# Seven-product units of a squared-ReLU MLP: where relu, squares and low halves stand in the order of two engines

## What is computed

```python
def sq_relu_mlp(h, w_up, w_down):
    return jnp.square(jax.nn.relu(h @ w_up)) @ w_down
...
        x = x + g1 * y_x
        h2 = modulate(rmsnorm(x, norm2_g[l]), sh2, sc2)
        x = x + g2 * sq_relu_mlp(h2, w_up[l], w_down[l])
```

## Time and profile before

| what | value |
|---|---|
| median of 3 runs | 1730.41 us |
| the three runs | 1732.12, 1727.40, 1730.41 us |
| the profiled execution's own time | 1729.16 us |
| its span, first to last instruction | 1727.4 us |
| mean granted TensorE clock | 0.970 |
| busy: TensorE (PE) | 1631.7 us, 94% |
| busy: VectorE (DVE) | 1273.7 us, 74% |
| busy: ScalarE (ACT) | 919.3 us, 53% |
| busy: GpSimd (POOL) | 255.6 us, 15% |
| DMA | 322.89 MB, mean 187 GB/s |

### The profile page before, as it was taken

How to read it: one execution, slowest core, us unless ns; L and a number is a source line. 1 busy time by engine, 2 the same in 40 slices (tenths; PEclk the granted TensorE clock), 3 DMA queues, 4 the chain that set the end, 5 groups by cost and what they waited for, 6 DMA issues and landing times.

```text
span 1727.4 us, 20083 instructions
## 1 busy us (share of the span) xinstructions
PE 1631.7 (94%) x8178; PEld 1321.9 (77%) x8178; DVE 1273.7 (74%) x1457; ACT 919.3 (53%) x1070; POOL 255.6 (15%) x176
## 2 busy tenths in 40 slices
PE   5999998999999898989999999889999999999994
PEld 2768876657988788887988687778888888888883
DVE  7544875877667646474699975479999898999984
ACT  6423235443443524253633234477878888888884
POOL 0000030000037131320000100021221212122110
PEclk9999998999999999999999998999999999999997
DMA  9106721003131223223122110289999999999993
GB/s 383 66 4 245 292 79 74 0 0 144 52 122 67 105 74 104 92 77 118 50 98 74 50 50 30 98 330 411 378 370 375 372 370 370 357 374 360 381 365 116
DMA packets 54482, 322.89 MB, mean 187 GB/s; under 512 B 12529, under 2 KB 13041, under 8 KB 17778
## 3 DMA queue, kind: packets, MB, share of 16 engines
q1 hardware_dynamic: 42192, 304.76, 46.2%
q0 software_dynamic: 9216, 8.43, 2.2%
q10 hardware_dynamic: 2978, 8.37, 1.2%
HBM read 323.60 MB, written 23.07 MB: 201 GB/s over the span
## 4 chain that ended last, share of the span: by engine, by line
PE 79%; DVE 10%; ACT 5%; DMA 3%; issue 2%; SPq 0%; POOL 0%; ACTq 0%; POOLq 0%; DVEq 0%
PE ps L584 25%; PE ps L1437 19%; PE ps L1464 10%; PE ps L763 4%; DVE blo L2274 2%; PE ps L739 2%; PE ps L1326 2%; PE ps L1002 2%; DVE scr L2475 2%; PE ps L796 1%; PE ps L1423 1%; DVE wlo L2165 1%; ACT whi L1515 1%; DMA xT<-in_x 1%; DVE scr L2274 1%
## 5 line engine op out<-in xcount | busy, mean ns | idle before, releaser
L2165 DVE TENSOR_TENSOR wlo<-raw,whi 128x2048 fp32r<-128x2048 f32 x256 | 585.3, 2307 | 146.4 <-ACT whi L1515 146.2
L1515 ACT ACTIVATE whi<-raw 128x2048 fp32r<-128x2048 f32 x256 | 485.2, 1910 | 142.6 <-PE ps L584 41.6
L1437 PE MATMUL ps<-whi,xH 128*128 128x512 f32 x512 | 205.2, 401 | 2.0 <-DVE xL L2274 2.0
L1437 PE MATMUL ps<-whi,xL 128*128 128x512 f32 x512 | 201.3, 393 | 0.0
L1437 PE MATMUL ps<-wlo,xH 128*128 128x512 f32 x512 | 199.9, 390 | 0.0
L584 PE MATMUL ps<-hH,whi 128*128 128x512 f32 x352 | 140.7, 400 | 0.3 <-ACT dmax L1980 0.3
L584 PE MATMUL ps<-hL,whi 128*128 128x512 f32 x352 | 139.2, 395 | 0.0
L584 PE MATMUL ps<-hH,wlo 128*128 128x512 f32 x352 | 139.1, 395 | 0.0
L3210 POOL DMA_INDIRECT sum_scratch<-yb,idt x32 | 51.1, 1595 | 454.6 <-ACT yb L2105 449.3
L1437 PEld LDWEIGHTS ps<-whi,xL 128*128 128x128 f32 x512 | 96.4, 188 | 22.5
L1437 PEld LDWEIGHTS ps<-whi,xH 128*128 128x128 f32 x512 | 96.7, 189 | 21.3 <-DVE xL L2274 2.3
(11 more groups left out here) (514 smaller groups left out, 3533.2 us busy)
## 6 DMA issues: line engine op xcount, KB each, us to landing
raw<-in_experts SPq DMA_DIRECT2D x192, 1024.0 KB, 7.7
raw<-in_streamed SPq DMA_DIRECT2D x92, 1024.0 KB, 4.8
xT<-in_x SPq DMA_DIRECT2D x1, 2048.0 KB, 17.2
h_scratch<-hN ACTq DMA_DIRECT2D x4, 512.0 KB, 2.6
sum_scratch<-xN ACTq DMA_DIRECT2D x1, 2048.0 KB, 13.8
out<-Y SPq DMA_DIRECT2D x4, 512.0 KB, 2.7
ctxT<-in_ctx SPq DMA_DIRECT2D x1, 1024.0 KB, 18.7
Y<-sum_scratch SPq DMA_DIRECT2D x2, 512.0 KB, 5.6
```

Source lines behind the costliest of these rows:

```text
L1437: ins = e.matmul(b.t[:, :], l, w, start=(kk == 0 and i == 0), stop=(kk == 7 and i == 2))
L1515: e.activation(u.hi, u.raw, ACT.Copy).then_inc(*p.inc("hi", n, on="hi"))
L2165: e.tensor_tensor(u.lo, u.raw, u.hi.bitcast(F32), ALU.subtract).then_inc(*p.inc("lo", n, on="lo"))
```

## The change

On ScalarE, relu and squares of unit c move into unit c+1: relu behind high half g+11 of the later unit, the squares behind its `p1s`. The high halves up to g+12 now stand ahead of `p1s`, and those up to g+17 behind the squares. In the fourth unit its own relu and squares follow at the end. On VectorE the low halves go up to g+10 ahead of the unit's first wait, to g+12 behind `u2s` and to g+14 ahead of `c1221`, in place of up to g+17 by the end. TensorE, GpSimd and SyncE are not changed, and no instruction or DMA is added or taken away.

```diff
@@ act_program, mlp
+        def positive(ch, c):
+            p.wait_ge(*done("dve", "c1221", ch, c))
+            e.activation(quad, quad, ACT.Relu).then_inc(*p.inc("r", ch, c))
+
+        def squared(ch, c):
+            p.wait_ge(*done("act", "r", ch, c))
+            p.wait_ge(*done("pe", "chunk", ch - 1))
+            e.activation(UH[:, 2 * c:2 * c + 2, :], scr[:, :, :], ACT.Square).then_inc(*p.inc("uh2", ch, c))
+            e.activation(quad, quad, ACT.Square).then_inc(*p.inc("us", ch, c))
+
         def seven(ch, c, n):
             g = STEP_AT[n]
+            ready(g + 11)
+            if c:
+                positive(ch, c - 1)
+            ready(g + 12)
             p.wait_ge(*done("pe", "block", n, 1))
             if n != U_UP[1][0]:
                 p.wait_ge(*done("dve", "c11", *((ch, c - 1) if c else (ch - 1, 3))))
             copy(p1s, ps["a", ch, c].t[:, 0:256], p.inc("p1s", ch, c))
-            for j in range(6):
-                ready(g + j + 11)
-            p.wait_ge(*done("dve", "c1221", ch, c))
-            e.activation(quad, quad, ACT.Relu).then_inc(*p.inc("r", ch, c))
-            p.wait_ge(*done("act", "r", ch, c))
-            p.wait_ge(*done("pe", "chunk", ch - 1))
-            e.activation(UH[:, 2 * c:2 * c + 2, :], scr[:, :, :], ACT.Square).then_inc(*p.inc("uh2", ch, c))
-            e.activation(quad, quad, ACT.Square).then_inc(*p.inc("us", ch, c))
+            if c:
+                squared(ch, c - 1)
             ready(g + 17)
+            if c == 3:
+                positive(ch, c)
+                squared(ch, c)
@@ dve_program, mlp
         def seven(ch, c, n):
             g = STEP_AT[n]
             a, b, d, f = (ps[x, ch, c].t for x in "abdf")
-            ready(g + 11)
+            ready(g + 10)
             p.wait_ge(*done("pe", "block", n, 1))
             p.wait_ge(*done("act", "p1s", ch, c))
             TT(u2s, a[:, 256:512], p1s, ALU.add, "u2s", ch, c)
@@
                             ALU.add).then_inc(*p.inc("w34", ch, c))
-            ready(g + 13)
             p.wait_ge(*done("dve", "w34", ch, c))
             TT(quad[:, 768:1024], b[:, 0:256], w34[:, 1, :], ALU.add, "c22", ch, c)
-            ready(g + 14)
             p.wait_ge(*done("pe", "block", n, 4))
             TT(quad[:, 0:256], d[:, 0:256], p1s, ALU.add, "c11", ch, c)
-            ready(g + 15)
-            ready(g + 16)
+            ready(g + 14)
             p.wait_ge(*done("pe", "block", n, 6))
             TT(quad[:, 256:768], f[:, :], sqs[:, :], ALU.add, "c1221", ch, c)
-            ready(g + 17)
             if c == 3:
                 lower_pair(ch, c)
```

## The result

The changed kernel takes 1704.82 us (median of 4 runs, 1701.89 to 1705.23), the kernel before 1730.81 beside it: ratio 0.9849, 95% interval 0.9831 to 0.9867. The forecast was 1704.2. Measured again later, it took 1703.87 us beside 1730.67, ratio 0.9842 (0.9828 to 0.9856); one of its six runs, which took 2341.01 us at a granted clock of 0.647, is left out of both.

What follows compares the result with a forecast made beforehand. TensorE carries 79% of the chain; it loses 8.54 + 8.67 + 8.97 = 26.2 us at three up-to-down switches. 1729.16 - 26.2 = 1703.0, and 1704.2 for the median, which lay 1.25 higher; range 1699.5 to 1716.

Steps and rivals of the forecast that it cites:

- The loss of 26.2 us at three switches: Where each chunk's up half ends and down half begins, TensorE idles, then runs slowly: 8.54, 8.67 and 8.97 us.
- the term for the slow matmuls: First 48 down matmuls of each chunk, partly at 1.2 GHz: 2.20, 2.30 and 2.63 us lost.
- 26.2 out, 0 in.: Whole kernel: the loss at the three switches goes, 26.2 us, and the moved work adds nothing.
- the rest moves forward as a block: Behind the sevens stage the chain stays on TensorE, so everything there was to come earlier unchanged.
- T6: Theory of a follow-up, not the prediction: VectorE's shorter reach costs a little, ScalarE's order alone 1 us or more faster.
- The tracing: Hand-traced VectorE times, chunk 1: first down low half at 583.0, wanted 586.35; last UL at 593.9, wanted 594.5.
- GpSimd's fourth sum: In units with sums, VectorE and GpSimd take turns, each turn costing VectorE one GpSimd sum, 1.3 us.
- Margins: Chunk 1: first down low half ready at 583.0 for 586.35; last UL just fits with 0.6 us to spare.
- ScalarE's waits: Sign in the changed profile: ScalarE's relu, which waited 6.64 us for VectorE's additions, waits under 3 us.
- Rival B (half comes): Last low half or first down half late in some chunk, TensorE waits: 1705 to 1718 us, middle 1708; chance 0.19.
- Rival C (VectorE sets the pace): Port shared with GpSimd slows VectorE to 12.8 us a unit against TensorE's 9.86: slower, 1737 us; chance 0.05.

Runs made afterwards that it cites:

- ul_x2: The changed kernel with each UL of the seven-product units made twice, one behind the other: 1706.21 us, ratio 0.986.
- high17: The kernel before with one edit on ScalarE, high half g+17 moved ahead of relu from behind the squares: 1713.95 us, ratio 0.9903.
- dve_only: The kernel before with only VectorE's part of the change, ScalarE keeping its old order: 1715.49 us, ratio 0.991.
- ul_x3: The changed kernel with each UL of the seven-product units made three times: 1730.57 us, ratio 0.9998.
- act_only: The kernel before with only ScalarE's part of the change, VectorE keeping its old order: 1703.73 us, ratio 0.9847; again later 1703.22 us.

## Why the prediction was right, point by point

- **The loss of 26.2 us at three switches.** The idle time and the slow matmuls are gone entirely, at all three. Two switches gave 8.45 each where I had 8.54 and 8.67. From the plain matmuls ahead of the sevens to those behind them (chain pieces at 514.45 and 788.99 before, 514.86 and 763.74 after) 274.5 us have become 248.9, so all three gave 25.7. What was mis-sized is the term for the slow matmuls. I set 13.08 us, which run from the first matmul's start to the end of the last one's record (0.39), against 48 pitches of 0.2267: the 0.16 by which a record is longer than its pitch was counted as loss, 0.5 us for three chunks.
- **"26.2 out, 0 in."** Between the two profiled executions the span fell by 24.2, from 1727.4 to 1703.2, and the medians by 26.0. That the forecast of 1704.2 lies within 0.6 of the measured 1704.82 is in part luck: the interval of the ratio is 3 us wide to each side, and two small errors lie inside it. One is the 0.5 us above. The other is my sentence that the rest moves forward as a block, which was not quite true. Behind the sevens stands a norm with a pause of TensorE, and there the clock was low for longer than before. Stretches before, then after, columns as in the earlier trace rows:

```profile
821.60:824.40 2.80, 2.80 (x14) 2.80 (x14) 0.59 (x2) 0.26 (x1) 0.00 (x0) 0.50 0.02 6
824.40:828.00 3.60, 3.60 (x29) 3.47 (x28) 2.60 (x6) 1.65 (x4) 0.00 (x0) 0.94 0.00 0
```

```profile
796.20:799.00 2.80, 2.80 (x14) 2.80 (x15) 0.59 (x2) 0.26 (x1) 0.00 (x0) 0.50 0.03 6
799.00:802.50 3.50, 3.50 (x20) 3.32 (x20) 2.01 (x5) 1.23 (x3) 0.00 (x0) 0.63 0.00 0
```

  Behind the same first stretch, 29 matmuls pass in 3.6 us before and 20 in 3.5 us after: about 1 us lost in this execution. From the first L692 piece of this norm to the first of L739 the chain takes 7.4 us before and in both profiled executions of ScalarE's order alone, and 8.7 in both of the changed kernel. That is the size of the difference which T6 went after; whether it is more than chance two executions of each do not show.
- **The tracing.** Chunk 1: low half of the first down unit: 583.0 forecast, 580.07 measured. Last UL: 593.9 against 592.06. VectorE's lateness in the second unit: 6.6 us forecast, 3.0 measured (`c1221` ends at 570.10, the next unit's first matmul starts at 567.09). The term that was mis-sized is GpSimd's fourth sum. I let it go ahead of low half g+14 in each unit. In the trace VectorE's next low half, standing ready, went first and took 0.69 us, and the sum took 1.69 where 1.3 is its shortest. So in each of the two units VectorE did not lose a turn of about 1.2 us that I had charged. The price of a turn was right: a UL beside a sum, which the trace of before did not show, took 2.34 us where I had 1.23 to 2.52. In chunk 2, counted from its first product at 630.30, the low half was ready at 32.7 and the last UL at 44.7, forecast 32.5 and 44.3.
- **Margins.** Forecast 3.3 and 0.6 us in chunk 1, measured 6.7 and 2.9. I had the fourth unit's last addition end 3.2 us behind its product; it was 0.9, with VectorE waiting for the product. That the last UL is the narrower one was right, and ul_x2 and high17 show TensorE stopping at exactly that place, k=6.
- **ScalarE's waits.** I said that the relu waits would be under 3 us; the one of the fourth unit is 3.70 in each chunk, because it waits for TensorE's own last product.
- **Rival B (half comes)** did not happen and is what dve_only and high17 do: 15.4 and 16.9 us faster than the 1730.84 beside them.
- **Rival C (VectorE sets the pace)** is real at a distance. It takes 2.5 us more on VectorE per unit, and then the kernel is back at 1730.57. I had its place right, UL at k=6, but looked only at the units with sums. By my own sum VectorE's work in a unit with nothing in its way is 7.6 us; with 2.5 more it is above TensorE's 9.86, so lateness is not made up where GpSimd is idle. In chunk 1 of ul_x3 the last additions end 5.6 us behind their product in the second unit, 5.9 in the third and 7.3 in the fourth; in the changed kernel it is 3.0, 0.9 and 0.9. The Trainium skill (SBUF — State Buffer, "Who interferes with whom") has the pair locked for a whole instruction by the first comer; the rows agree (a UL of one shape takes 1.23 us alone and 2.21 to 2.34 beside a sum).
- **What the prediction did not separate** is the two halves. ScalarE's alone gives the whole gain, VectorE's alone 15.4 us of it, and VectorE's on top of ScalarE's nothing in time.

## What to carry to other kernels

When two engines each show long idle times that end on the other, look at what stands in front of the awaited instruction in its queue: here a 0.6 us conversion stood behind 3 us of work that itself waited. Let work that waits for another engine's result lag by one unit, and put independent work ahead of it. Then measure the room with a repeated instruction: a schedule that gains 26 us and one that gains none lay 2.5 us of VectorE work per unit apart. And look at what a margin hangs on: the rooms of 6.7 and 2.9 us here stayed the same when VectorE had less to do, because each begins with something that VectorE and ScalarE wait for TensorE to finish.

## What was not expected of the hardware

A wait of TensorE of about 2 us brings the clock down in one chunk and not in the next, in one execution. In dve_only it waits the same 1.85 to 1.86 us ahead of each down half. The stretches behind these waits:

```profile
590.00:591.00 1.00, 1.00 (x4) 0.71 (x4) 1.00 (x2) 0.00 (x0) 0.00 (x0) 0.50 0.68 123
...
676.00:680.00 4.00, 3.96 (x17) 3.30 (x18) 3.97 (x6) 0.00 (x0) 0.00 (x0) 1.00 0.70 250
...
684.00:686.00 2.00, 0.50 (x3) 0.07 (x1) 1.19 (x1) 2.00 (x2) 0.14 (x1) 1.00 0.61 254
...
763.00:768.00 5.00, 4.97 (x15) 3.92 (x16) 4.96 (x7) 0.00 (x0) 0.00 (x0) 0.66 0.57 210
```

The granted clock is 0.50 (1.2 GHz) in chunk 1 and 0.66 on the mean in chunk 3, and full in chunk 2; high17's waits of 2.2 us at k=6 were followed by the full clock in all three. In dve_only the low clock cost nothing on balance. At full clock, in chunk 2, TensorE comes to k=6 early and waits 1.59 us there for the last UL (the stretch at 684), so the 48 matmuls with their waits take 12.9 us in chunk 2 as in chunks 1 and 3. So it does not explain why dve_only scatters more (1712.92 to 1717.64) than act_only (1701.56 to 1704.59). In high17 the wait lies at k=6 itself and nothing behind it would hide a low clock; whether that is behind its scatter (1708.92 to 1716.38) was not tested.

The other one is that the expert stage, which lies far behind the sums and has no part in them, took 7 to 8 us longer in the two kernels that left most of the sums out.
